# The moving blocks of x, t and the raw weights begin at another byte of their 128-byte line

## What is computed

```
x = x + 0.5 * swiglu_ffn(rms_norm(x, ffn1_norm), ffn1_w_in, ffn1_w_out)       # d_ff 2816
h = rms_norm(x, mix_norm)
q, k, v, xr, gate = split(h @ w_in_proj)                                       # 3*512 + 2*512
y_attn = diff_attention(q, k, v, ...)      # 4 heads, two softmax maps each, chunk-causal
y_rnn  = rg_lru_branch(xr, gate, ...)      # conv of width 4, block gates, linear scan, gelu
x = x + concat([y_attn, y_rnn]) @ w_out_proj
x = x + 0.5 * swiglu_ffn(rms_norm(x, ffn2_norm), ffn2_w_in, ffn2_w_out)

def swiglu_ffn(h, w_in, w_out):
    g, u = split(h @ w_in)
    return (silu(g) * u) @ w_out
```

## Time and profile before

| | us |
|---|---|
| three runs | 888.19, 888.19, 890.52 (median 888.19) |
| the profiled execution | 888.08 |
| its span, first to last instruction | 886.3 |
| TensorE matmuls busy | 880.4 (99%) |
| TensorE weight loads busy | 789.1 (89%) |
| VectorE busy | 673.5 (76%) |
| ScalarE busy | 492.3 (56%) |
| GpSimd busy | 73.0 (8%) |

### The profile page before, as it was taken

The page is one execution under the profiler, slowest core; times in us unless marked ns, Lnnn a source line. Parts: engine busy times, 40 slices in busy tenths (PEclk is TensorE's granted clock), DMA queues, the critical chain, the costliest instruction groups (busy, mean ns, idle before and its releaser), DMA issues.

```text
span 886.3 us, 14865 instructions
## 1 busy us (share of the span) xinstructions
PE 880.4 (99%) x5564; PEld 789.1 (89%) x5564; DVE 673.5 (76%) x1211; ACT 492.3 (56%) x832; POOL 73.0 (8%) x105
## 2 busy tenths in 40 slices
PE   8999999999999999999999999999999999999998
PEld 7899988999999888888887788999988999999887
DVE  6999763888886567876889889999744788887342
ACT  7877521676664334456657667777522567765120
POOL 0111000121110000000000000112000112110000
PEclk9999999999999999999999999999999999999999
DMA  7568523777674333322220123767533677775340
GB/s 260 169 167 193 133 89 113 197 186 186 173 195 123 105 107 131 113 78 95 95 96 1 48 96 92 174 172 213 122 119 106 166 193 189 187 178 143 107 130 36
DMA packets 28125, 121.37 MB, mean 137 GB/s; under 512 B 3376, under 2 KB 4016, under 8 KB 20784
## 3 DMA queue, kind: packets, MB, share of 16 engines
q1 hardware_dynamic: 16128, 87.79, 28.8%
q0 software_dynamic: 11664, 32.51, 19.9%
q10 hardware_dynamic: 288, 0.52, 0.2%
HBM read 86.74 MB, written 2.10 MB: 100 GB/s over the span
## 4 chain that ended last, share of the span: by engine, by line
PE 97%; DVE 1%; DMA 1%; ACT 0%; SPq 0%; issue 0%; ACTq 0%
PE bank L1644 32%; PE bank L1646 31%; PE bank L1645 31%; PE bank L1901 1%; PE bank L1924 1%; DMA raw<-w_in_dram 1%; PE bank L1914 0%; PE bank L1835 0%; DVE o L1608 0%; DVE w_lo L994 0%; ACT probs L939 0%; ACT sq L919 0%; PE bank L1659 0%; SPq L473 0%; DVE w_lo L1403 0%
## 5 line engine op out<-in xcount | busy, mean ns | idle before, releaser
L1644 PE MATMUL bank<-t_hi,w_hi 128*128 128x256 f32 (+1 forms) x856 | 250.7, 293 | 1.1 <-DVE w_lo L1403 0.9
L1646 PE MATMUL bank<-t_hi,w_lo 128*128 128x256 f32 (+1 forms) x856 | 249.7, 292 | 0.0
L1645 PE MATMUL bank<-t_lo,w_hi 128*128 128x256 f32 (+1 forms) x856 | 249.4, 291 | 0.0
L1644 PEld LDWEIGHTS bank<-t_hi,w_hi 128*128 128x128 f32 x856 | 160.7, 188 | 6.5 <-DVE w_lo L1403 1.4
L1646 PEld LDWEIGHTS bank<-t_hi,w_lo 128*128 128x128 f32 x856 | 161.0, 188 | 3.8
L1645 PEld LDWEIGHTS bank<-t_lo,w_hi 128*128 128x128 f32 x856 | 160.3, 187 | 4.1
L571 ACT ACTIVATE w_hi<-raw 128x1024 fp32r<-128x1024 f32 (+2 forms) x102 | 85.1, 882 | 127.5 <-PE bank L1646 127.5
L1644 PE MATMUL bank<-act_hi,w_hi 128*128 128x512 f32 (+1 forms) x364 | 139.2, 382 | 0.0
L1646 PE MATMUL bank<-act_hi,w_lo 128*128 128x512 f32 (+1 forms) x364 | 139.2, 382 | 0.0
L1645 PE MATMUL bank<-act_lo,w_hi 128*128 128x512 f32 (+1 forms) x364 | 139.1, 382 | 0.0
L994 DVE TENSOR_TENSOR w_lo<-raw,w_hi 128x1024 fp32r<-128x1024 f32 (+2 forms) x98 | 94.2, 1002 | 9.6 <-ACT w_hi L571 9.2
(11 more groups left out here) (235 smaller groups left out, 1609.6 us busy)
## 6 DMA issues: line engine op xcount, KB each, us to landing
raw<-w_in_dram SPq DMA_DIRECT2D x43, 1024.0 KB, 4.8
w_lo<-raw POOLq DMA_DIRECT2D x42, 512.0 KB, 5.5
w_lo<-raw POOLq DMA_DIRECT2D x38, 256.0 KB, 3.3
raw<-w_out1b_dram SPq DMA_DIRECT2D x8, 768.0 KB, 4.5
raw<-w_qkv_dram SPq DMA_DIRECT2D x6, 1024.0 KB, 4.8
raw<-w_out2b_dram SPq DMA_DIRECT2D x8, 768.0 KB, 4.4
raw<-w_out1a_dram SPq DMA_DIRECT2D x8, 640.0 KB, 3.8
raw<-w_out2a_dram SPq DMA_DIRECT2D x8, 640.0 KB, 3.9
```

The costliest lines, as they stand in the source:

```text
L1644: pe.matmul(dst, s_hi, m_hi, start=first, stop=False, skip_group_check=added)
L1645: pe.matmul(dst, s_hi, m_lo, start=False, stop=False, skip_group_check=added)
L1646: return pe.matmul(dst, s_lo, m_hi, start=False, stop=last, skip_group_check=added)
```

## The change

One constant goes from 64 to 96. It is added to the byte offset of `t_lo`, `t_hi`, `x`, `raw` and the `q_parts`. No instruction is added, removed or reordered, and no size changes.

```
-        ACT_AT, T_LO_AT, T_HI_AT, X_AT, RAW_AT, T_SHIFT = 20, 50, 66, 82, 90, 64
+        ACT_AT, T_LO_AT, T_HI_AT, X_AT, RAW_AT, T_SHIFT = 20, 50, 66, 82, 90, 96
```

## The result

The changed kernel took 897.83 to 898.16 us in four runs, median 897.87; the kernel before, in four runs beside them, 888.19 to 890.52, median 889.27. The ratio is 1.0089 with a 95% interval of [1.0075, 1.0103]. The forecast was 897.5. The profiled execution took 897.83 us with a span of 896.0 (before 888.08 and 886.3): +9.7 us of span.

A forecast was written before the change was run, and what follows sets the result against it. TensorE's matmul pitch was taken to bound the kernel. Seven-product matmuls +9.3 us, plain matmuls, helpers and DMAs 0, gave 897.4 us against the profiled 888.08, or 897.5 against the median 888.19; range 875 to 900 us.

The forecast's parts named there:

- The bound: Whole kernel: TensorE busy 880.4 of 886.3 us, no wait worth removing; time is number of matmuls times pitch.
- The seven-product term: 3192 matmuls moving t blocks, now at 96 instead of 64: pitch 120.0 ns in all groups, +9.3 us.
- the upper bound: Seven-product matmuls: 120.0 ns pitch in all four groups, together +9.3 us; the end taken for the forecast.
- Why 120: Seven-product matmuls: 96 moves toward the 120 ns row, and the fast rhythm looks like an exception easily lost; called weak.
- The plain term: 288 matmuls of 512 columns on t: taken as 0, bounds -0.6 to +0.6 us.
- VectorE, ScalarE, DMAs: Helpers using raw, x and t at the new place: taken as 0, any small delay hidden behind TensorE.
- Rival C: Loads and adds so slow that operation 1 waits in each of 38 chunks: 13.7 us, 901.9 us; chance 0.02.
- The rule on 16-byte lines: Memory accesses: 64 and 96 are both multiples of 16, so nothing changes, 888.2 us; doubted from the trace.
- A: Faster seven-product groups: 113.3 ns everywhere, 875.6 us; only one long group, 883.7; chance 0.36 with partial form.
- today's mean pitch: Seven-product groups before the change: mean 117.2 ns over 3192 matmuls, used to set the threshold for a 0.3% gain.
- the lower end of 875: Bottom of the forecast range in us, from 875.6 - 0.6 for the fast rhythm everywhere with its plain part.

## Why the prediction was right, and where its reason was not

*The bound.* Right: TensorE's pitch sets the time, no helper and no wait took part, and the sum over the matmuls gives the growth of the span.

*The seven-product term.* Right in size: +9.3 us forecast, +8.9 measured, pitch 120.0 ns in every chunk without a gap, as at the upper bound. The 0.4 us lie in the third group, where the gaps before and after weren't the same: they came to 0.3 ns x 672 = 0.2 us instead of 0.7.

*Why 120.* Here the argument was lucky. That 96 lies near a multiple of 128 is no reason: 32 lies as near and has 116.7. What holds is what the rows before already hinted at, that the place against the weights counts, and the run with everything moved by 32 together, which costs nothing, shows it. That the cost arises beside the weight load is supported by the run with half a load (116.7 for 120.0), which changes the outputs written as well. By which order of accesses 0 and 96 come to 120.0, 48 to 118.3, 32 to 116.7 and 64 to one of two levels stays open. At 64 a group can have either rhythm, which before the change the first group showed against the second; at 0, 32, 48 and 96 each profiled group found a single level, at 80 two, even within one group. What picks the rhythm stays open too.

*The plain term.* This term was mis-sized: I took 0 with bounds of -0.6 and +0.6 us, from the belief that 96 can cost at most as much over 64 as 64 over 0. Measured were 4 ns for each of 288, +1.2 us, 0.8 of it seen in the span. The 229 ns of before were no fixed price of 64 either: at 64 the same matmuls have 229 ns in one stretch and 233 in another, so the row stood for one of two rhythms.

*VectorE, ScalarE, DMAs.* Right at zero: the adds still land after 5.5 and 3.3 us, the loads after 4.8, and a sum of two blocks of raw takes 684 ns for 686. Rival C had no part, and x and raw at 96 alone did not change the time.

*The rule on 16-byte lines.* The Trainium skill, "Advanced Engine Details and Errata", section SBUF Cachelines, speaks of lines of 16 bytes and names no cost of where a block begins; by it 0, 32, 48, 64, 80 and 96 would have been equal. The runs show 113.3 to 120.0 ns among them; its lines can't be the whole matter. The Trainium skill, "SBUF — State Buffer", section Who interferes with whom, gives TensorE two read ports, one for the moving operand and one for weight loads, calls them independent, and says that TensorE never waits on anyone. By that, moving the one against the other would change nothing; measured are 116.7 ns at 32 and 120.0 at 96, and the half-load run fits that TensorE's own two reads get in each other's way.

*The chances.* A had 0.36 and in its full form needed 113.3 ns everywhere. That was never seen in all groups at any place tried, and A's price was too high besides: the third group at 192 gained 2.0 us by the fast rhythm and not 3.0. Two slips of the working change nothing: today's mean pitch is 117.3 ns and not 117.2, and the lower end of 875 takes off the plain part twice. The luck can be priced: had 96 cost what 32 does, the time would have been about 888.3, no change, and the same argument would have forecast 897.5.

## What to carry to other kernels

Where matmuls of few columns follow each other with a full weight load for each, compute the pitch from start to start, group by group, and compare it between groups of equal shape: two levels at equal addresses are a reason to suspect that the load and the moving block read in each other's way. Then try the four places that 32-byte steps allow within 128 bytes, moving the moving block against the weights, since nearness to the weights' place doesn't tell the order; a place with one steady level can be worth as much as one that is sometimes better. Judge a place by every group of a trace and by several runs, since the rhythm differs between them.

## What the runs showed of the hardware that I had not expected

- A shift of 32 bytes between the moving block and the weights is worth up to 3.3 ns in 120 (116.7 at 32, 120.0 at 0 and 96), with nothing but addresses changed; a shift of 16 bytes 1.6 ns (118.3 at 48).
- At a distance of 64 the same 84 matmuls run at 113.3 or 117.8 ns, and which of the two differs from group to group and from trace to trace: +2.2 us for the first group alone. At 80 it changed from 118.3 to 120.0 inside one group.
- Even in matmuls of 512 columns, where the loads are busy only 16.4 of 20 us, the place matters: 227 ns at 0, 229 or 233 at 64, and 233 at 32 and 96. It is another order than with 256 columns, where 0 and 96 show no difference and 32 is better than both.
